# A hybrid S5 / linear-attention layer on one Trainium2 core: opening reordered, adaLN sums placed between matmuls, down jobs split 384 + 384, row groups in the attention products

## What is computed

```python
ml = jnp.split((jax.nn.silu(c) @ ada_w[i] + ada_b[i])[:, None, :], N_MOD, axis=-1)
mc = jnp.split((jax.nn.silu(c_ctx) @ ada_w[i] + ada_b[i])[None, None, :], N_MOD, axis=-1)
...
def ffn_sublayer(t, shift, scale, gate, norm_g, w_gate, w_up, w_down):
    h = modulate(rms_norm(t, norm_g), shift, scale)
    return t + gate * (MACARON_WEIGHT * swiglu(h, w_gate, w_up, w_down))
...
        z = glr[..., d * GLA_GATE_RANK:(d + 1) * GLA_GATE_RANK] @ gate_up[d] + gate_b[d]
...
    return (o_intra + o_inter).reshape(bsz, nh, l, dv), s_final
```

## Time and profile before

| | us |
|---|---|
| median of 3 runs | 1388.96 (1388.0 to 1392.38) |
| profiled execution | 1395.53 |
| span of it | 1393.8 |
| TensorE busy | 1357.1 (97%) |
| VectorE / GpSimd / ScalarE busy | 864.4 / 638.7 / 397.3 |
| mean granted clock of TensorE | 0.988 |

### The profile page before, as it was taken

How to read it: one execution, slowest core, us unless ns; L and a number is a source line. 1 busy time by engine, 2 the same in 40 slices (tenths; PEclk the granted TensorE clock), 3 DMA queues, 4 the chain that set the end, 5 groups by cost and what they waited for, 6 DMA issues and landing times.

```text
span 1393.8 us, 21125 instructions
## 1 busy us (share of the span) xinstructions
PE 1357.1 (97%) x8432; PEld 1219.2 (87%) x8432; DVE 864.4 (62%) x1319; ACT 397.3 (29%) x739; POOL 638.7 (46%) x400
## 2 busy tenths in 40 slices
PE   5799999999999999999999999999999999999997
PEld 3699998999999999997887888888898999999996
DVE  4874566857755656437556349944768756555666
ACT  3320010110110111024635141132141455554454
POOL 1362443543533434432631418635647355665561
PEclk9799999999999999999999999999999999999999
DMA  9632344345245245213321378775646133334321
GB/s 359 174 112 68 116 132 141 103 127 157 90 127 172 66 137 171 61 50 106 78 61 39 69 206 223 206 216 186 190 135 196 46 110 103 92 113 121 101 89 63
DMA packets 236654, 178.10 MB, mean 128 GB/s; under 512 B 33353, under 2 KB 211725, under 8 KB 236557
## 3 DMA queue, kind: packets, MB, share of 16 engines
q1 hardware_dynamic: 216368, 145.65, 36.3%
q10 hardware_dynamic: 20188, 31.11, 6.8%
HBM read 156.86 MB, written 19.86 MB: 127 GB/s over the span
## 4 chain that ended last, share of the span: by engine, by line
PE 90%; DVE 6%; ACT 1%; DMA 1%; issue 1%; SPq 0%; DVEq 0%; ACTq 0%
PE ps L1197 44%; PE ps L1872 13%; PE ps L1484 10%; PE ps L1933 7%; PE ps L1487 4%; PE ps L1206 1%; PE ps L1747 1%; PE ps L1415 1%; PE ps L1784 1%; DVE ada_acc L2688 1%; PE ps L1711 1%; PE ps L1366 1%; PE ps L1715 1%; DVE scaled L3139 1%; DMA x_in<-in_ctx_dram 1%
## 5 line engine op out<-in xcount | busy, mean ns | idle before, releaser
L1103 POOL TENSOR_SCALAR w_hi<-w_raw 128x1024 fp32r<-128x1024 f32 x128 | 152.7, 1193 | 569.6 <-PE ps L1197 298.1
L1106 POOL TENSOR_TENSOR w_lo<-w_raw,w_hi 128x1024 fp32r<-128x1024 f32 x128 | 321.6, 2512 | 10.7
L1197 PE MATMUL ps<-h_hi,w_lo 128*128 128x384 f32 (+2 forms) x1000 | 290.7, 350 | 0.5 <-DVEq L3246 0.5
L1197 PE MATMUL ps<-h_lo,w_hi 128*128 128x384 f32 (+2 forms) x1000 | 286.8, 346 | 0.0
L1197 PE MATMUL ps<-h_hi,w_hi 128*128 128x384 f32 (+2 forms) x1000 | 286.5, 346 | 0.0
L1197 PEld LDWEIGHTS ps<-h_hi,w_lo 128*128 128x128 f32 x1000 | 178.7, 188 | 16.3 <-issue 5.3
L1197 PEld LDWEIGHTS ps<-h_hi,w_hi 128*128 128x128 f32 x1000 | 180.9, 188 | 10.9
L1197 PEld LDWEIGHTS ps<-h_lo,w_hi 128*128 128x128 f32 x1000 | 180.9, 188 | 9.9
L1179 POOL TENSOR_TENSOR w_lo<-w_raw,w_hi 128x512 fp32r<-128x512 f32 x90 | 116.0, 1302 | 105.4 <-ACT w_hi L2457 103.9
L2688 DVE SCALAR_TENSOR_TENSOR ada_acc<-ada_w,cs,ada_acc 128x1024 f32<-128x1024 f32 x70 | 110.2, 1608 | 9.6 <-DMA ada_w<-in_ada_w_dram 7.6
L1872 PE MATMUL ps<-h_hi,w_hi 128*128 128x256 f32 x360 | 102.0, 283 | 0.0
(11 more groups left out here) (450 smaller groups left out, 2803.3 us busy)
## 6 DMA issues: line engine op xcount, KB each, us to landing
w_raw<-in_ffn_w_gate_dram SPq DMA_DIRECT2D x44, 512.0 KB, 4.8
w_raw<-in_ffn_w_up_dram SPq DMA_DIRECT2D x44, 512.0 KB, 4.0
w_raw<-in_ffn_w_down_dram SPq DMA_DIRECT2D x44, 512.0 KB, 4.1
ada_w<-in_ada_w_dram ACTq DMA_DIRECT2D x32, 512.0 KB, 4.0
w_raw<-in_w_in_dram SPq DMA_DIRECT2D x32, 512.0 KB, 4.0
ada_w<-in_ada_w_dram SPq DMA_DIRECT2D x30, 512.0 KB, 4.5
c_scr<-cp ACTq DMA_DIRECT2D x16, 288.0 KB, 3.8
b_scr<-bt_sb ACTq DMA_DIRECT2D x16, 256.0 KB, 3.7
```

Source lines behind the costliest of these rows:

```text
L1103: pool.tensor_scalar(w_hi[:, s, 0:cols], w_raw[:, s, 0:cols], 1.0, 1.0, ALU.mult, ALU.mult)\
L1106: pool.tensor_tensor(w_lo[:, s, 0:cols], w_raw[:, s, 0:cols], w_hi[:, s, 0:cols].bitcast(F32), ALU.subtract).then_inc(w_split, 1)
L1197: last = pe.matmul(mv[2], st, mv[part], start=(first and q == 0), stop=(n == len(terms) - 1 and q == 2))
```

## The change

1. **Opening.** `PLAIN` = 4 tiles are formed on VectorE as x times the roots before the scale's columns are there; ScalarE multiplies them by `amul` in place. The other four tiles take three steps on VectorE instead of two, since the roots now lie in two banks of 384. PE runs half of row1's products before the roots are spread, and turns lambda before it waits for the copy of row0. GpSimd splits unit 2, and so unit 3, after all eight tiles of `h_lo`.
2. **Sums.** In the last gate/up job of the first segment one of the sixteen sums stands behind each pair of matmuls from k = 2 on. They go to the second bank of the slot of job v = 6.
3. **Down jobs** of the first FFN split the 768 columns 384 + 384; VectorE adds in three steps. Their order is k = 0 to 2 with e = 0 to 2, then e = 3, then the last k of all four (in both FFNs).
4. **Logits.** Columns 384 to 767 of `glr` lie in partitions 64 to 127, with a second copy of `gate_up` (eight DMAs); the two matmuls use different rows of the array. `glr` is evacuated in three steps.
5. **Readout.** Per token group both heads' 128-row matmuls come first, then the eight quarter products with heads alternating.

```diff
@@ -121,6 +121,7 @@
+PLAIN = KD // 2
@@ -458,10 +459,10 @@
-    glr = mix("glr", [4 * RANK, NT])
+    glr = mix("glr", [P, NT])
...
-    gate_up = mix("gate_up", [4 * RANK, 2, KEY])
+    gate_up = mix("gate_up", [P, 2, KEY])
@@ -638,6 +639,12 @@
+    def down_banks(j, two_banks):
+        if two_banks:
+            return [(both(j, 384)[:, b, :], slice(384 * b, 384 * b + 384)) for b in range(2)]
+        return [(lat(j), slice(0, NL))]
@@ -649,6 +656,10 @@
+    def ada_ctx_cols(j):
+        return ctx_(j)[:, ADA_COL:ADA_COL + 2 * KD].rearrange("p (t v) -> p t v", v=2)
@@ -1132,6 +1143,8 @@
                         if fresh and n < 4:
                             is_done(pool, JOB["row1"])
+                            if n == 2:
+                                pool.wait_ge(h_ok, KD)
@@ -1182,7 +1195,7 @@
-            def split_mm(terms):
+            def split_mm(terms, between=None):
@@ -1196,6 +1209,8 @@
+                        if between:
+                            between(n, q)
@@ -1219,48 +1234,57 @@
-            def row_products(g):
+            def row_products(g, k0=0, k1=KD):
...
-                wait_read(pe, j)
-                for k in range(KD):
+                if k0 == 0:
+                    wait_read(pe, j)
+                for k in range(k0, k1):
...
                     for q in range(2):
...
-                last.then_inc(job_done, 1)
-            def turn_row(g):
+                if k1 == KD:
+                    last.then_inc(job_done, 1)
+            def turn_row(g, jobs):
...
+                last.then_inc(job_done, jobs)
+            def spread_roots():
+                j = JOB["spread"]
+                wait_read(pe, j)
+                pe.wait_ge(root_inv, 1)
+                for t in range(6):
+                    o = both(j, 384)[:, t // 3, P * (t % 3):P * (t % 3) + P]
+                    last = pe.matmul(o, root[:, t:t + 1].to_broadcast([P, P]), ident[:, :], start=True, stop=True)
...
+            def turn_lambda():
+                j = JOB["lam"]
+                pe.wait_ge(small_in, 16 * SMALL)
+                wait_read(pe, j)
...
-            row_products(1)
+            row_products(1, 0, 4)
+            spread_roots()
+            row_products(1, 4)
...
-            turn_row(1)
+            turn_row(1, 1)
...
+            turn_lambda()
...
-            turn_row(0)
...
+            turn_row(0, 3)
@@ -1292,6 +1316,11 @@
+            def ada_sum(cols, g, n):
+                t, v = n // 2, n % 2
+                pe.matmul(cols[:, t, v:v + 1], ada_vec(g, v)[:, P * t:P * t + P], ones[:, 0:1], start=True, stop=True)
@@ -1456,13 +1485,20 @@
-                        last = split_mm(terms)
-                        if two and g and v == (1 if nth else 2 * tiles - 1):
-                            if is_folded(g):
-                                last = folded_sums(ada_sum_cols(j), g)
-                            else:
-                                pe.wait_ge(acc_ok, ada_added(g, KD))
-                                last = ada_sums(ada_cols(j, ADA_COL), g)
+                        if two and nth == 0 and v == 2 * tiles - 1:
+                            def sums_between(k, r):
+                                n = 3 * (k - 2) + r
+                                if n == 0:
+                                    slot_free(js.down(2))
+                                    pe.wait_ge(acc_ok, ada_added(ADA_START, KD))
+                                if 0 <= n < 2 * KD:
+                                    ada_sum(ada_ctx_cols(js.gu(v - 1)), ADA_START, n)
+                            last = split_mm(terms, sums_between)
+                        else:
+                            last = split_mm(terms)
+                        if two and nth and g and v == 1:
+                            last = folded_sums(ada_sum_cols(j), g)
@@ -1481,11 +1517,9 @@
                         for r, (st, mv) in enumerate(((wl, act_hi), (wh, act_lo), (wh, act_hi))):
-                            last = pe.matmul(lat(j), st[:, k, c], mv[:, k, 0:NL], start=(k == 0 and r == 0),
-                                             stop=(k == tiles - 1 and r == 2))
-                            if two:
-                                last = pe.matmul(ctx_(j)[:, 0:NC], st[:, k, c], mv[:, k, NL:NT],
-                                                 start=(k == 0 and r == 0), stop=(k == tiles - 1 and r == 2))
+                            for bank, cols in down_banks(j, two):
+                                last = pe.matmul(bank, st[:, k, c], mv[:, k, cols], start=(k == 0 and r == 0),
+                                                 stop=(k == tiles - 1 and r == 2))
@@ -1518,10 +1552,20 @@
                     step = lat_step if part.late else down_step
-                    for k in range(tiles):
+                    def act_here(k):
...
-                        for e in range(4):
+                    for k in range(tiles - 1):
+                        act_here(k)
+                        for e in range(3):
+                            if two and part.segs + i == 0 and e == 2 and k == 0:
+                                pe.wait_ge(gu_ok, tiles)
...
+                    act_here(tiles - 1)
+                    for k in range(tiles - 1):
+                        step(3, k)
+                    for e in range(4):
+                        step(e, tiles - 1)
@@ -1641,11 +1685,12 @@
                 for q in range(2):
-                    last = pe.matmul((lat, ctx_)[q](j)[:, 0:384], gate_up[:, d, P * ti:P * ti + P],
-                                     glr[:, 384 * q:384 * q + 384], start=True, stop=True)
+                    r = slice(64 * q, 64 * q + 64)
+                    last = pe.matmul((lat, ctx_)[q](j)[:, 0:384], gate_up[r, d, P * ti:P * ti + P], glr[r, 0:384],
+                                     start=True, stop=True)
...
-            pe.wait_ge(small_in, 16 * (SMALL + 4))
+            pe.wait_ge(small_in, 16 * (SMALL + 8))
@@ -1705,17 +1750,17 @@
                         hd = 2 * ti + hp
-                        r = slice(64 * hp, 64 * hp + 64)
-                        o = (lat, ctx_)[hp](j)
...
-                            pe.matmul(o[:, 0:DV], at_sb[:, dd, hp, t, :], v_sb[:, t, DV * hd:DV * hd + DV],
+                            pe.matmul((lat, ctx_)[hp](j)[:, 0:DV], at_sb[:, dd, hp, t, :], v_sb[:, t, DV * hd:DV * hd + DV],
...
+                    for dd in range(2):
...
-                            for dd in range(2):
-                                last = pe.matmul(o[64 * par:64 * par + 64, 0:DV],
+                            for hp in range(2):
+                                r = slice(64 * hp, 64 * hp + 64)
+                                last = pe.matmul((lat, ctx_)[hp](j)[64 * par:64 * par + 64, 0:DV],
...
-                                                 stop=(par == 1 and dd == 1), skip_group_check=True)
+                                                 stop=(dd == 1), skip_group_check=True)
@@ -2006,6 +2051,12 @@
                 act.sem_inc(row_ok, 1)
+                if g == 1:
+                    act.wait_ge(cols_ok, 1)
+                    for k in range(PLAIN):
+                        for c, v in ((slice(0, NL), 0), (slice(NL, NT), 1)):
+                            ins = act.activation(scaled[:, k, c], scaled[:, k, c], ACT.Copy, scale=amul[:, 0, k, v:v + 1])
+                        ins.then_inc(xn_ok, 1)
@@ -2190,9 +2241,14 @@
             act.wait_ge(gla_c, 1)
...
-                for r in (RANK * d, RANK * (2 + d)):
+                for r in (RANK * d, RANK * (2 + d), RANK * (4 + d), RANK * (6 + d)):
...
-            evac_tokens(JOB["glr"], glr[:, :], NT, 4 * RANK)
+            j = JOB["glr"]
+            is_done(act, j)
+            src = lat(j)[0:64, :].rearrange("p (r w) -> p r w", w=GRID_W)
+            act.activation(w_major(glr[0:64, 0:384]), src[:, :, 0:48], ACT.Copy)
+            act.activation(w_major(glr[64:P, 0:P]), src[:, :, 48:64], ACT.Copy)
+            act.activation(glr[64:P, P:384], ctx_(j)[0:64, 0:NC], ACT.Copy).then_inc(slot_read[j % 4], 1)
             for q in range(2):
@@ -2974,7 +3030,7 @@
-                                ada_bias(ada_cols(ju, ADA_COL), ada_summed(nth))
+                                ada_bias(ada_ctx_cols(jg), ada_summed(nth))
@@ -3020,10 +3076,12 @@
                         j = js.down(k)
                         done(j)
...
-                        ins = STT(x[:, k, 0:NL], lat(j), mod[:, g, 0:1], x[:, k, 0:NL], ALU.mult, ALU.add)
...
-                            ins = STT(x[:, k, NL:NT], ctx_(j)[:, 0:NC], mod[:, g, 1:2], x[:, k, NL:NT],
-                                      ALU.mult, ALU.add)
+                            for src, c, v in ((lat(j)[:, 0:384], slice(0, 384), 0), (ctx_(j)[:, 0:NL - 384], slice(384, NL), 0),
+                                              (ctx_(j)[:, NL - 384:384], slice(NL, NT), 1)):
+                                ins = STT(x[:, k, c], src, mod[:, g, v:v + 1], x[:, k, c], ALU.mult, ALU.add)
+                        else:
```

(17 more changed lines are left out.)

16 lines of the change are left out of this document (3 added, 13 removed).

## The result

| | before | after |
|---|---|---|
| median, 20 runs each | 1392.66 us | 1382.71 us |
| lowest and highest | 1388.0 / 1394.98 | 1377.4 / 1388.82 |
| profiled execution | 1395.53 | 1379.35 |
| span of it | 1393.8 | 1377.6 |
| mean granted clock of TensorE in it | 0.988 | 0.996 |

The account below looks back on a forecast made before the run. TensorE, busy 97% of the span, was taken as the bound. Opening 7.0, sums 4.2, down split 4.2 and linear attention 5.0 made 20.4 us, taking the median from 1389.0 to 1368.6, range 1360 to 1380 (8 in 10).

Parts of the forecast that it names:

- the attention term: Linear attention, logits and readout together: a gain of 5.0 us, from 0 to 7.5.
- the stall called 0 at v = 5 and ahead of the sums: First segment's gate/up jobs: TensorE's new waits for VectorE or ScalarE cost nothing, up to 1.5 and 2 us.
- the price of a down pair before: Side segment's down phase, first FFN: a 512 + 256 pair taken at 0.3567 us, against 0.3456 to 0.3475 for 384 + 384.
- Opening, 7.0 (3.2 to 9.2): Start to the joint jobs' end: earlier turning and h_lo and less half clock gain 7.0 us, 3.2 to 9.2.
- Sums, 4.2 (0 to 6.3): Sixteen adaLN sums before the first down phase: 3.8 saved, 2.1 paid between matmuls, 2.5 of clock won; 4.2 us.
- 16 x 0.13: Last gate/up job, first segment: sixteen inserted sums at 0.13 us each, 2.1 us, bounded by 0 and 0.237 each.
- rival 1: Opening keeps its half clock and the inserted sums bring the low clock again: 13.9 us gained, 1375; chance 0.17.
- Down split, 4.2 (3.0 to 5.0): First FFN's down jobs: 384 + 384 pairs cheaper over 480 pairs, less 0.3 for VectorE's third add; 4.2 us gained.
- Logits, -0.6 and +0.9: Linear attention logits: first eight matmuls lose 0.6 us net after a 2.0 stall, the two later fours gain 0.9.
- rival 2: Linear attention gives nothing: late loads stall the logits, ScalarE holds both readouts; 15.4 us gained, 1373.6; chance 0.12.
- Readout, 4.7: Linear attention readout: two heads in 1.75 us for 2.48, 5.9 over eight blocks, less 1.2 waiting for ScalarE.
- Rival 3: VectorE takes TensorE's place: later splits delay its chain, some 4 us of wait at v=5; 16.4 gained, 1372.6; chance 0.08.

Follow-up runs that it names:

- second profile of before: The kernel before, unaltered, run and profiled again: the profiled execution took 1393.2 us at a clock of 0.990, the slowest of twelve (1387.0 to 1393.2).

## Why the prediction was wrong

**What failed, in short.** The forecast gain has two kinds of terms. By its own bounds 6.3 of the 20.4 us are clock: 3.8 in the opening (7.0, where 3.2 would come with the whole half clock) and 2.5 at the sums. The other 14.1 are instructions and waits: 3.2 opening, 1.7 sums, 4.2 down split, 5.0 attention. Measured over all runs, the means differ by 8.6: 1.0 by the clock (0.9923 to 0.9931 at 1.2 us for 0.001) and 7.7 at equal clock. So both failed, the instructions and waits by 6.4 us and the clock by 5.3. Only the attention term held: 5.6 for 5.0. The steps that failed are the stall called 0 at v = 5 and ahead of the sums, the price of an inserted sum, the price of a down pair before, and a clock credit read from one execution.

**The time it starts from.** The clock terms were read from one execution, 1395.5 us at 0.988, and then taken off the median. Moved to a clock of 0.995 that execution is at 1387.1, with the others (1387.7), so the clock explains all of its distance. A usual run, at 0.9923, has some 1.2 x 4.3 = 5.2 us less clock loss, and what it has less the change can't save once more. The comparison of the two profiles hides this: before at 0.988 and after at 0.996, it holds some 9.6 us of clock, more than the 6.3 forecast, and only about 7 of instructions and waits. Its 16.2 is near the forecast by luck. Besides, the median to which the gain was applied, 1389.0 from three runs, became 1392.7 with twenty, and this puts 3.7 us more between the forecast time and the measured one.

**Opening, 7.0 (3.2 to 9.2).** The steps came as said (37.1 for 37.9; h_lo at 49.0 for 50; 59.3 for 60.6), 8.3 us between the profiles. The half clock in it was 3.4 to 6.8 us in all traces with the new opening but that with the dummies, also as said. Yet in medians the opening alone gives 0.1 and 0.5 us, in means 1.5 against all runs of before, at equal clock nothing. The second profile of before shows why. Its joint jobs end 5.8 us later than the changed kernel's; it has 10.2 us more of half clock there, which cost 4.7 at 0.46. So 1.1 are left for the steps themselves, not 3.2, and the new waits, 0.43 at v = 5 and 0.99 ahead of the sums, take those. Both stand where the prediction said that a new wait would prove it wrong. As for the clock, usual runs of before had less of it to give back than the two profiled ones (with the opening alone the mean clock rises from 0.9923 to 0.9940, worth 2.0 us), and with the sums between the pairs a third of the runs now lose it there. How much an execution of before at 1387 us loses in its opening is not traced. VectorE's chain at v = 5 did not move (84.66 for 84.80). I had that margin, 7.9 us, and called the stall 0; it was 0.43, and 1.1 in the trace with the dummies. I had also said that VectorE's chain would be a little earlier; the load behind the moved units kept it.

**Sums, 4.2 (0 to 6.3).** The term 16 x 0.13 was mis-sized. Timeline after:

```profile
105.19 0.38 PE L1323 MATMUL ps<-ones,ada_acc 128*128 128x1 f32 x2 [0.99 <-ACT silu L2143]
105.43 0.60 PE L1210 MATMUL ps<-h_lo,w_hi 128*128 128x384 f32 x2
105.87 0.28 PE L1323 MATMUL ps<-ones,ada_acc 128*128 128x1 f32 x2
...
106.44 0.28 PE L1323 MATMUL ps<-ones,ada_acc 128*128 128x1 f32 x2
```

From sum to sum 0.573 us, less a pair at 0.347: 0.226 each, near the 0.237 of the block, the upper bound I gave. Nothing is hidden; 3.6 us, not 2.1. The clock term, 2.5 in favour, came in the profiles of the upper level: none of the changed kernel's has half clock in the first down phase. But it has another side. In eleven of 31 runs of the changed kernel the mean clock is at or below 0.991, and in the three profiles of its relatives at their lower level (0.991, 0.989, 0.993) 17 to 20 us of half clock lie on the sums and cost 8 to 9. That was rival 1's mechanism, on the side of the sums alone; it left a gain of 1.5 us where in such a run some 8 are lost. That the changed kernel itself, at its lower level, loses it in the same place is inferred, not traced.

**Down split, 4.2 (3.0 to 5.0).** The step that failed is the price of a pair before: 0.3567 came from the whole phase, with its start. In the middle 24 matmuls take 4.24 us, 0.3533 a pair, and 4.16 after, 0.3467. 480 x 0.0066 = 3.2; 2.3 in the milestones, as each side segment loses 0.14 again in its gate/up jobs, and 1.7 in the runs. The 0.3 set off for the third add is of that size, though where the 0.14 goes is not shown. (The lower figure less 0.3 is also 4.1, not 4.2.) The down order saved nothing, as said.

**Logits, -0.6 and +0.9.** The products gained 1.24 (1.4 forecast) and 0.64 twice (0.45). The wait was 3.38 us, not 2.0: it ended on the loads, not on the evacuation, as the eighth was issued at 661.4 beside a 512 KB weight load and came 3.6 us later. In two other profiles of the changed kernel the wait is 1.3 and 3.1, with no half clock behind it. I had the issue time right (4.53 for 5.0) and no price for the landing. Behind the wait of 3.38 us 3.42 us of half clock cost some 1.6. These terms add up to a loss of 2.4 in this execution, rival 2's first half. From the end of the first FFN to the first readout the three profiles stand at 3.1 lost, 1.3 lost and 0.5 gained against before, so it is a matter of the execution; over all runs, at equal clock, 0.4 are lost.

**Readout, 4.7.** Right in mechanism and better than said: 3.12 twice, 6.2. The 1.2 us for ScalarE's third take-out did not come; it started at 751.21, before TensorE had done with the turns and scores.

**Rivals and range.** The changed kernel's better level, 1379, lies in the range, its median not. Rivals 1 and 2 together, 1380, were the upper end; of each only a part came, the low clock on the sums in a third of the runs and the late loads. Rival 3's mechanism, VectorE in TensorE's place, came in small. No rival had the instruction terms of opening, sums and down split too large all at once, and that is as much of the miss as the clock. I took the clock as one stretch that a change either removes or not, with 3 us at stake, and not as a scatter of 7 us between runs of one kernel, which three runs of before (1388.0 to 1392.4) and one at 1395.5 already showed.

**At equal clock** the parts, each from its own runs, come to -6.0 (readout), -1.7 (down), -0.1 (sums), +0.5 (opening), +0.4 (logits): -6.9, and the whole is -7.7. The difference is within their errors (0.2 to 0.4 each).

## What to carry to other kernels

Before a gain is taken from a profile, compare the profile's mean clock with that of other runs: what the profiled execution lost to the clock beyond the median can't be won from the median, and a profile of before at a low clock beside one of after at a high clock shows a gain that the runs don't have. Price clock and instructions apart, and give the clock its scatter. Where an opening is made faster, follow the other engines' chains behind it to the first place where TensorE waits for them, and the loads that stand behind what was moved. An issue of eight small loads needs the price of their landing under traffic, not only of their issue.

## What the runs showed of the hardware

- A one-column fp32 matmul between pairs of 384 columns costs 0.226 us, as much as alone (0.237). TensorEngine Tiling (Array Packing) of the Trainium skill, Instruction Overhead, has one column cost as much as sixty; by it, as an estimate, the two passes of a sum would take 0.05 us at 2.4 GHz. These runs show more, and issuing the sums twice added 3.9 us to the median, 0.24 each.
- The half-clock stretches in these traces lasted 3.41, 6.83, 10.24, 13.65, 17.07 and 20.48 us. One of 17.07 lay on the sums between dense pairs and on the start of the down phase in one execution (the changed kernel with the old logits, 1384.9), and four of the eight runs of that kernel, at 1376.2 to 1377.6 and 0.996 to 0.997, can't have had it. What decides was not found: idle of 1 us ahead is not needed (0.46 in one such trace), and issuing the sums twice brought the lower level in four runs of ten, not in most.
- Filling the idle of the opening with dummy transposes took its half clock away in the one trace, and the mean clock of the runs rose (0.9973 for 0.9956); the median did not fall.
- 64-row matmuls in two row groups ran 8 in 1.54 us for 2.77; four-quadrant work with one change of shape for two heads took 1.68 us for 2.48.
- Small VectorE steps take very different times: one copy of 128 x 64 took 0.20, 0.92 and 2.24 us in three traces, and TensorE waited 2.18 us behind the longest. What lengthens it was not found.
- A low mean clock is not new with the change: 42 of 98 runs of before are at or below 0.991, and in its two traces the half clock lies in the opening and in the first down phase. With sums between the pairs but the old opening 0 of 18 runs are, with both 20 of 71. So whether the long stretch ever falls on the sums without the new opening stays open.
